# One block for attention and mixing: V stationary, outputs kept turned, weights of the softmax applied on GpSimd, ten expert units fetched before the experts

## What is computed

```python
def nsa_core(q, ..., gates, kc, vc, kc_end, ks_blk, vs_blk, kw, vw, kw_pos):   # 8 heads of 64, 2 KV heads
    p_c = masked_softmax(s_c, kc_end <= t);  o_c = p_c @ vc      # compressed blocks: 31 of them
    p_s = masked_softmax(s_s, mask_s);       o_s = p_s @ v_sel   # selected blocks (all, for 512 tokens)
    p_w = masked_softmax(s_w, mask_w);       o_w = p_w @ vw      # sliding window of 512
    return gates[..., 0:1] * o_c + gates[..., 1:2] * o_s + gates[..., 2:3] * o_w

def finish(x, y_pool, o_nsa, o_mem, p):
    mixed = concat([rmsnorm(y_pool, g[:256]), rmsnorm(o_nsa, g[256:768]), rmsnorm(o_mem, g[768:])])
    h = x + mixed @ p['w_out']                     # 1024 x 1024
    hn = rmsnorm(h, p['g_ffn'])
    return h + hier_moe(hn, p)                     # top 1 of 4 groups, then top 2 of 8 experts
```

## Time and profile before

| | us |
|---|---|
| median of 3 runs | 1144.41 |
| lowest, highest | 1142.44, 1147.15 |
| the profiled execution, whole | 1142.65 |
| its span, first to last instruction | 1140.8 |
| blocks in the span: project_and_stream / attend / mix / experts, start | 0 / 338.1 / 495.1 / 643.0 |

### The profile page before, as it was taken

The page is one execution under the profiler, slowest core; times in us unless marked ns, Lnnn a source line. Parts: engine busy times, 40 slices in busy tenths (PEclk is TensorE's granted clock), DMA queues, the critical chain, the costliest instruction groups (busy, mean ns, idle before and its releaser), DMA issues. The chain is left out here.

```text
span 1140.8 us, 13984 instructions
## 1 busy us (share of the span) xinstructions
PE 941.3 (83%) x5663; PEld 555.7 (49%) x5663; DVE 343.4 (30%) x788; ACT 169.1 (15%) x403; POOL 108.7 (10%) x130
## 2 busy tenths in 40 slices
PE   4899969998768999978994599987777777777875
PEld 2455535555447777764554355544343434343432
DVE  3222252313436587733345211111011101110110
ACT  1111131211114344410111000000000000000000
POOL 0000123221000000000000111111110111011111
PEclk9899969999887698878995699999999999999998
DMA  9762036669016000062325489999999999999992
GB/s 391 296 192 70 14 105 153 142 136 231 10 36 252 1 1 2 1 250 119 111 84 215 179 349 411 414 416 416 413 420 415 414 412 420 408 413 412 418 386 73
DMA packets 63976, 273.66 MB, mean 240 GB/s; under 512 B 10448, under 2 KB 26639, under 8 KB 38111
## 3 DMA queue, kind: packets, MB, share of 16 engines
q1 hardware_dynamic: 50135, 255.70, 57.5%
q0 software_dynamic: 7376, 12.85, 4.1%
q10 hardware_dynamic: 6400, 4.20, 1.8%
HBM read 266.16 MB, written 19.10 MB: 250 GB/s over the span
## 5 line engine op out<-in xcount | busy, mean ns | idle before, releaser
L1952 PE MATMUL ps<-w_a,xTe 128*64 128x256 f32 x640 | 78.5, 393 | 28.0 <-DMA w_a<-in_w_up 14.7
L1952 PE MATMUL ps<-w_b,xTe 128*64 128x256 f32 x640 | 76.7, 384 | 25.7 <-DMA w_b<-in_w_up 15.6
L434 PE MATMUL ps<-w_b,front 128*128 128x454 f32 (+1 forms) x240 | 81.6, 551 | 0.7 <-ACT z L407 0.7
L1862 POOL DMA_INDIRECT out_y<-yb,halves x32 | 50.0, 1564 | 297.0 <-ACT yb L2074 297.0
L1952 PEld LDWEIGHTS ps<-w_a,xTe 128*64 128x64 f32 x640 | 45.7, 140 | 58.0 <-DMA w_a<-in_w_up 21.0
L1952 PEld LDWEIGHTS ps<-w_b,xTe 128*64 128x64 f32 x640 | 44.4, 136 | 55.0 <-DMA w_b<-in_w_up 22.8
L2074 ACT ACTIVATE yb<-ps,slot_w 128x512 f32<-128x512 f32 x32 | 22.0, 687 | 287.1 <-PE ps L1977 283.1
L2033 DVE SCALAR_TENSOR_TENSOR gc<-gc,ps 128x256 f32<-128x256 f32 x32 | 13.5, 421 | 163.4 <-ACT gc L2068 163.4
L883 PE MATMUL ps<-front,w_a 128*128 128x378 f32 x192 | 62.0, 482 | 0.0
L1507 PE MATMUL ps<-w_b,xg 128*128 128x512 f32 x128 | 58.3, 615 | 1.9 <-ACT xg L1577 1.3
L1952 PE MATMUL ps<-z,xTe 128*64 128x256 f32 x384 | 45.8, 384 | 16.5 <-DMA z<-in_w_up 8.4
(11 more groups left out here) (361 smaller groups left out, 1323.8 us busy)
## 6 DMA issues: line engine op xcount, KB each, us to landing
w_a<-in_w_gate SPq DMA_DIRECT2D x20, 1024.0 KB, 28.0
w_a<-in_w_up SPq DMA_DIRECT2D x20, 1024.0 KB, 28.2
w_a<-in_w_down SPq DMA_DIRECT2D x20, 1024.0 KB, 28.6
w_b<-in_w_gate SPq DMA_DIRECT2D x20, 1024.0 KB, 28.1
w_b<-in_w_up SPq DMA_DIRECT2D x20, 1024.0 KB, 28.7
w_b<-in_w_down SPq DMA_DIRECT2D x20, 1024.0 KB, 28.0
w_a<-in_cache_kv SPq DMA_DIRECT2D x64, 256.0 KB, 5.6
z<-in_w_gate SPq DMA_DIRECT2D x12, 1024.0 KB, 28.1
```

Source lines behind the costliest of these rows:

```text
L434: ins = nc.tensor.matmul(in_psum(t, a), xT[:, t % 2, k, 0:r], rhs, start=(k == 0), stop=(k == KD - 1))
L1862: pool.indirect_dma_start(out=rows, out_offset=bass.IndirectOffsetOnAxis(ap=self.halves[:, n:n + 1].bitcast(U32), axis=0), in_=yb[:, slot, ...
L1952: ins = nc.tensor.matmul(ps[h * CAP:h * CAP + CAP, bank, 0:FH], xT[:, n // 2 % 2, k, CAP * slot:CAP * slot + CAP], w[:, k, h * FH:h * FH + ...
```

## The change

- `attend` and `mix` stand in one block, `attend_and_mix`, with no barrier between them. Their buffers lie in `front`, which is no longer freed, and the probabilities in `w_a`. The ring places 8 and 9 are the start of `front`.
- **Values.** The work is cut in two sequences. 30 units are scored as before (order cmp, sel, mem, win). 28 "values" (t, kind, k) are turned and multiplied: for sel and win one for each block k of 128 keys with all four heads, `(t+1)` of each kind for a tile. V is stationary (64 columns), the turned probabilities move with 512 columns, and the two KV heads write to the lower and upper 64 partitions of one bank. The result has channels on the partitions and is kept so in `mT`. No zero products are needed. `pT` has two buffers, `stt` six.
- **Weighing.** DVE's `factor` makes only the reciprocal times the gate; POOL multiplies the probabilities (`weigh`). PE's turn(v) waits for `weighed` of the last unit it needs.
- **Pooling** is at the front of the attention: window products for all four tiles, four small products with 512 columns, squares by ACT, their sum over channels by a product with a matrix of ones (`pool_ssq`), before the first score is turned.
- **Norms.** For each tile POOL squares the six turned chunks, PE sums them with ones (`ssq`), DVE scales (`ms`), ACT takes the root, DVE the reciprocal and six scalings (`scale`), all a few values later in the loop; for the last tile beside the output projection of the first. The gains come as columns, by two DMAs of 1280 single elements.
- **Mixing.** The output projection takes `mT` as it is: the turning of `mixed` and its copy are gone. Its order of tiles is 0, 1, sample, 2, 3 (before 0, 1, 2, 3, sample).
- **Fetching.** SP issues units 0, 1, 2, 6, 7 after the last turning and the last value product; 3, 4 and 9 when the last projection is done; 8 after the last router product, 5 after the last logits. `experts` begins with unit 10.

```diff
+        def gpsimd(pool):
+            def weigh(u):
+                pool.wait_ge(factors, u + 1)
+                pr, f = prob(u), stt[:, u % 6, 3, 0:2 * n]
+                if n == 4:
+                    for j in range(2):
+                        ins = nc.gpsimd.tensor_tensor(pr[:, j, :, :], pr[:, j, :, :], f[:, 4 * j:4 * j + 4].unsqueeze(2).broadcast_to([P, 4, w]), ALU.mult)
+                else:
+                    for i in range(2 * n):
+                        ins = nc.gpsimd.tensor_scalar(pr[:, i // n, i % n, :], pr[:, i // n, i % n, :], f[:, i:i + 1], None, ALU.mult)
+                ins.then_inc(weighed, 1)
...
-                        v = V0 + 128 * (1 if kind == "sel" else 2) + 64 * j
-                        for i, r in enumerate(rs):
-                            for k in range(t + 1):
-                                ins = nc.tensor.matmul(ps[:, 6, 64 * c:64 * c + 64], pT[:, j, at:at + 128], z[:, k, v:v + 64], **add)
+                        V = V0 + 128 * (1 if kind == "sel" else 2) + 64 * j
+                        ins = nc.tensor.matmul(ps[hs, 6, :], z[:, k, V:V + 64], pT[:, v % 2, j, :], start=False, stop=(v == end_of[t]), skip_group_check=True)
...
+            windows()
+            pe.wait_ge(out_d, PRE_D)
+            score(0)
+            pool_proj()
+            score(1)
+            pool_ssq()
+            score(2)
+            for v in range(NV):
+                turn(v)
+                for u in issued(v):
+                    score(u)
+                value(v)
...
+            def scale(a):
+                dve.wait_ge(root_ready, a + 2)
+                    ch.then(nc.vector.reciprocal(rms[:, :, :], rms[:, :, :]))
+                for k in range(0 if a == 0 else 2, KD):
+                    ins = nc.vector.scalar_tensor_tensor(m, m, cols[:, k:k + 1], ..., ALU.mult, ALU.mult)
...
-                    sp.wait_ge(h_in_psum, TILES + 4)
-                    for u in range(3, 5):
+                    sp.wait_ge(h_in_psum, hcount[i])
+                    for u in (3, 4, 9):
                         self.load_unit(sp, u)
...
+            sp.wait_ge(l_in_psum, NT)
+            self.load_unit(sp, 8)
             sp.wait_ge(l_out, NT)
             self.load_unit(sp, 5)
...
-            for u in range(8, NU):
+            for u in range(RING, NU):
```

More of the change, by code:

```diff
@@ L1113, in attend @@
         NU = len(units)
-        opens = lambda u: u == 0 or units[u][0] != units[u - 1][0]
-        ends = lambda u: u == NU - 1 or opens(u + 1)
-        block = st.enter_context(nc.Block("attend"))
-        @block.sync
-        def _(sp):
+        values = [(t, kind, k) for t in range(TILES) for kind in ("cmp", "sel", "mem", "win") for k in range(t + 1 if kind in ("sel", "win") else 1)]
+        NV = len(values)
+        need = [max(u for u in range(NU) if units[u][0:2] == values[v][0:2]) for v in range(NV)]
@@ new lines, in attend @@
+        last_of = {values[v][0:2]: v for v in range(NV)}
+        end_of = [last_of[t, "win"] for t in range(TILES)]
+        ahead = []
+        for v in range(NV):
+            t, kind, k = values[v]
+            n = t + 1 if kind in ("sel", "win") else 1
+            after = v - k + n
+            span = (need[after] if after < NV else NU) - need[v]
+            ahead.append(min(NU, need[v] + 3 + span * k // n))
+        ahead.append(NU)
+        self.attend_sems = (valued, p_turned, o_out, normed, NV)
@@ new lines, in attend, with shape @@
+        issued = lambda v: range(ahead[v], ahead[v + 1])
+        before_u = {u: last_of[(t - (1 if kind in ("sel", "win") else 2), kind)] for u, (t, kind, _) in enumerate(units) if t >= (1 if kind in ("sel", "win") else 2)}
+        SAMPLE_AT = {"turn": 0, "raw": 1, "y": 2, "ys": 3, "sq": 3, "ssq": 4, "ms": 5, "scale": 6}
+        at = lambda what, v: [t for t in range(TILES - 1) if end_of[t] + {"out": 1, "sq": 1, "ssq": 2, "ms": 3, "scale": 4}[what] == v]
+        half = 256
+        def shape(u):
+            t, kind, rs = units[u]
+            return {"cmp": (4, NC_P, 32), "mem": (2, MEM, MEM)}.get(kind, (len(rs), (t + 1) * P, (t + 1) * P))
@@ L1219, in _ @@
+            windows()
+            pe.wait_ge(out_d, PRE_D)
             score(0)
+            pool_proj()
             score(1)
-            for u in range(NU):
-                if u + 2 < NU:
-                    score(u + 2)
-                if u >= 1:
-                    value(u - 1)
-                turn(u)
-            value(NU - 1)
-        def shape(u):
-            t, kind, rs = units[u]
-            return {"cmp": (4, NC_P, 32), "mem": (2, MEM, MEM)}.get(kind, (len(rs), (t + 1) * P, (t + 1) * P))
@@ L1321, in _ @@
-        @block.scalar
-        def _(act):
+            factor(0)
+            pool_ms()
+            peak(2)
+            factor(1)
+            nc.vector.memset(rms[:, 0, 0:96], 1.0)
+            for v in range(NV):
+                take(v)
+                for u in issued(v):
+                    peak(u)
+                    factor(u - 1)
+                    if u == NU - 1:
+                        factor(u)
+                if v == 1:
+                    pool_scale()
+                if v == SAMPLE_AT["raw"]:
+                    sample_raw()
+                if v == SAMPLE_AT["ms"]:
+                    ms(0)
+                if v == SAMPLE_AT["scale"]:
+                    scale(0)
+                for t in at("ms", v):
+                    ms(t + 1)
+                for t in at("scale", v):
+                    scale(t + 1)
@@ L1346, in _, with root @@
+            def root(a):
+                act.wait_ge(ms_ready, a + 2)
+                r = rms[:, 0, 0:96] if a == 0 else rms[:, :, :]
+                nc.scalar.activation(r, r, ACT.Sqrt).then_inc(root_ready, 1)
             exp(0)
             exp(1)
[L1348 to L1359 removed]
@@ L1367, in mix @@
+            out(TILES - 1)
+            root(TILES)
+        return st, (sync, gpsimd, vector, scalar, tensor)
     def mix(self):
@@ new lines, in mix @@
+        spread = self.sqT.rearrange("p k n -> p (k n)")
+        room, at = self.front[:, 4 * D + KD * NTOK:], 0
+        lg, ro, one, both, cnt, prod = (room[:, sum(ROUTE[:j]):sum(ROUTE[:j + 1])] for j in range(6))
+        lg = lg.rearrange("p (t n) -> p t n", t=NT)
+        ro = ro.rearrange("p (t n) -> p t n", t=NT)
+        one = one.rearrange("p (t k e) -> p t k e", t=NT, k=2)
+        both = both.rearrange("p (t e) -> p t e", t=NT)
+        cnt = cnt.rearrange("p (t e) -> p t e", t=NT + 1)
```

829 lines of the change are left out of this document (451 added, 378 removed).

## The result

The changed kernel takes 1152.49 us (median of 20 runs, 1147.44 to 1158.04). The kernel before, run 20 times beside it, takes 1141.97 (1132.18 to 1153.37). The ratio is 1.0111 with a 95% interval of 1.0084 to 1.0138: **1.1% slower**, where 1111 us were forecast. The profiled run took 1157.71, its span is 1155.8: 15.0 more than before.

A forecast was written before the change was run, and what follows sets the result against it. PE was taken to bound the attention and mixing, weight transfers the experts from unit 12 on. +18 - 21 - 30 + 0 = -33 gave 1109.7 us, 1111 against the median, range 1082 to 1138.

The forecast's parts named there:

- Part B: Attention loop: 119.5 us in place of 140.5, -21 us (0 to -38).
- PE's idle time: Attention loop: 5 of PE's 9.9 us of idle time gained, with bounds of +6 to -8.
- PE's work: Attention loop: about 95 us of PE work at 2.4 GHz, 114.5 us busy.
- value products: Attention loop: sel and win products with V stationary and 512 columns moving, a gain of 16 us (7 to 24).
- cmp: Attention loop: 32 products of 10.8 us become eight of 512 columns at 5.5 us, -5.
- zero products: Attention loop: these products of 3.0 us go, -3; the wait ahead of them brings net nothing to -4.
- POOL's price: Loop: weighing on POOL at 29 us by a copy's row; about three times slower before it falls behind.
- Rival 2: Attention loop: hand-overs eat the gain, the loop stays at 140, 1132 us in all; chance 0.14.
- Rival 4: Attention loop: turnings hold PE at its lower clock, +81 on the loop's 119.5, 1190 us in all; chance 0.10.
- Part A: Front of the attention: pooling ahead of the first turning delays the first `pT` copy, +18 us (12 to 24).
- Part C: Mixing: the gap ahead of the first projection and the turnings of `mixed` go, -30 us (-26 to -33).
- Part D: Ten units before the experts: unit 12 still waits for expert 0's down product, 0 (down to -10.7).

The follow-up runs named there:

- run 20: No label of a run but a count: the unchanged kernel before, run 20 times beside the changed kernel, median 1141.97 us.
- e9: Changed kernel with only the table of score issue made even, one or two units behind every turning and most scores earlier: 1135.6 us, ratio 0.992 to the kernel before.
- e5: Changed kernel with each value product issued behind the next turning on PE: 1150.2 us, ratio 1.011 to the kernel before.
- e6: Changed kernel with value products behind the next turning and POOL's multiplications all in two-operand form: 1139.8 us, ratio 0.999 to the kernel before.
- e10: e9 plus both edits of e6 (value product behind the next turning, two-operand form on POOL): 1127.7 us, ratio 0.987 to the kernel before.
- e14: e12 with the window products waiting for their own bands alone, not for all constants: 1122.4 us, ratio 0.982 to the kernel before.
- e2: Changed kernel with POOL multiplying only one column of each unit, the rest left unweighed: 1143.0 us, ratio 1.000 to the kernel before.
- e13: e10 with POOL multiplying only one column of each unit, the rest left unweighed: 1123.6 us, ratio 0.982 to the kernel before.
- e8: Kernel before with only the weighing moved to POOL: 1178.3 us, ratio 1.032 to the kernel before.
- e3: Changed kernel with every POOL multiplication as one with two tensor operands: 1147.1 us, ratio 1.004 to the kernel before.
- e1: Changed kernel with the weighing of the probabilities back on DVE: 1153.9 us, ratio 1.010 to the kernel before.
- e12: e10 with ACT's exponentials of a block's scores issued behind the next block's copy: 1128.1 us, ratio 0.987 to the kernel before.
- e4: Changed kernel with ring places 8 and 9 fetched at the start of the experts again: 1155.4 us, ratio 1.011 to the kernel before.

## Why the prediction was wrong

**Part B failed**, and in one step of it, PE's idle time: "I take -5 of PE's 9.9 us of idle time as gain". The loop was forecast at 119.5 us and took 174.8. PE's work was right: forecast 95 us at 2.4 GHz, measured 126.92 x 0.73 = 93; value products, cmp and zero products went as worked out. The miss of 55.3 us is 42.9 of idle time (47.9 for 5) and 12.4 of busy time at the lower clock (126.9 for 114.5). The bounds had the clock at 0.75 or more, just above what came, and idle time at 6 us more than before: it rose by 38.

The reason is that the term was taken from averages (busy 93% before, DVE's 94 us in 120, POOL's 29 us) and not from the order of the new loop. The order of instructions around the last tile showed blocks whose turning, score and product follow each other, and a table that issues four scores behind one turning and none behind the next three. The sentence "it has the stretch between two scores to work ahead" assumed even spacing. e9 shows that the old table costs 1.9% against the even and earlier one; e5 and e6 show the copy wait and POOL's rate covering for each other. Of the 55.3 us that the loop missed, e9 brings back 18.8 and e10 27.7; e14, the best, 32.0, its last step within the spread of the runs. So the cause is shown for about half of the miss.

**POOL's price** was wrong by a factor of 2.8: 29 us by the row of a copy, 80.4 by the trace (29.0 + 24.7 + 19.6 + 4.1 + 3.0). The prediction named the point from which that counts, three times a copy, and the 512-column form lies at 2.7. e2 prices it at 12 us in the changed loop, e13 at 4 in the even one (there with the two-operand form, 54 us of POOL), e8 at 35 in the kernel before.
The Trainium skill ("GPSIMD Engine Reference", 3.1) has 4497 ns for a two-operand operation of 2,048 columns, 2.2 ns a column, and the trace agrees for that form: 1042 ns for 512, 2.0 a column. Its section 4.1 calls one-operand work on GpSimd roughly line rate; here the form with one factor per partition took 1562 ns for 512, 3.1 a column, and was the slower of the two (e3), against 0.48 us on DVE (e1).

**Rival 2** (hand-overs eat the loop's gain) came nearest to the mechanism, at a chance of 0.14, and far too small: it was priced at "the loop stays at 140", 20.5 us over the forecast where 55.3 came, as if before's loop were its upper end. Nothing said that it was. **Rival 4** (the clock) forecast the slower side, but not for the reason that came: in the third tile e10 holds 0.83 and e12 0.91 with all the turnings, where the changed kernel has 0.73. The slower side came by idle time, with the clock behind it for 12 us. The row that rival 4 was built on, 380 to 400 at 0.52, hides what stood ahead of it: a stop of 2.64 us, behind which the zero products and the turnings ran at the lower level.

```profile
378.45 0.90 PE L1193 MATMUL ps<-zb 1*128 1x512 bf16 x2 [2.64 <-ACT o L1359]
379.15 3.51 PE L1200 MATMUL ps<-kcv,pT 31*128 31x64 f32 x16
382.59 1.97 PE L1183 MATMUL ps<-consts,xg 128*128 128x128 f32 x8
```

That stretch has three groups of eight turnings, the one at 1.00 (464 to 484) five.
The Trainium skill ("TensorE: Matmul & The Clock Gate", Part 4) says that the full clock does not engage for transposes; the rows of e10 and e12 speak against it as a rule for this loop.

**Part A** was +13.4 for +18, inside its bounds, on the time axis; counted from the block's first DMA (338.14 before, 336.44 after) it is +15.1. The window products did wait for constants, 3.85 us, but for the pooling state; the two DMAs of single elements had landed 5.9 and 6.3 us after their issue, the pooling state 6.7 after its own, later one. **Part C** was right, -32.5 for -30 with the last tile in it. To the last projection's end it is -35.8 for -31.7: PE's 2.03 us of idle time and its lower clock (0.95, worth 3.7 us, to 1.00) both went, where the prediction took 2.4 for the first projection. The last tile cost +3.3 for +2. **Part D** was right: 15.98 and 15.97 us from unit 10 to unit 12, and e4 the same time without the early fetch.

Open is what holds the last 23 us of the even loop (142.8 in e14 against 119.5). 34 us of it are idle, mostly PE behind DVE's copies (22.0 us in e14) and behind ACT's exponentials (10.2); e12 moved the wait for copies from ACT to DVE and didn't remove it. Against the kernel before, the first tile lost most: from one cmp turning to the next the four tiles take 22.2, 36.3, 36.1 and 47.8 us before (the last to the copy to `o`), and 33.4, 37.5, 38.7 and 38.8 in e14. So no loop of this case is shorter than before's 140.5, and what e9 to e14 gain on the kernel before comes from Part C. Why the clock is 0.71 with 21% idle time (e2) and 0.80 with 26% (e9) is open too: it does not go by the idle share.

## What to carry to other kernels

When an edit makes one step need the results of several earlier ones, look in the printed order for groups of producers ahead of it and for empty stretches behind: here at least a third of the loop's loss came from there (18.8 of 55.3 us), and no busy share showed it. Price a hand-over by the order of the new loop, with the longest chain between two instructions of the bounding engine, and don't take the old time as its upper end. If removing the suspected cost (e2) gives little, change the order before looking for a faster engine: the table of e9 gave more than any move of work.

## What the hardware showed

On GpSimd a multiplication of 512 columns by a factor per partition took 1562 ns, and one with a second tensor operand repeated along the columns 1040 ns. After a stop of 8.97 us PE came back at the lower level for three groups (turnings of 1.97 in place of 1.09 us), while gaps of 0.80 to 0.88 us between groups at the full level, from 503 to 514 us, left it there.
